# Two routers of a block with two expert layers: rows ahead of their mean, weights on four column tiles, token rows by ScalarE and GpSimd

## What is computed

```python
x = layer_norm(ALPHA * x + mix, ln_mix_g[l], ln_mix_b[l])
ffn = grouped_moe(x, router_w, router_bias, moe_w_gate[l], moe_w_up[l], moe_w_down[l])
x = layer_norm(ALPHA * x + ffn, ln_ffn_g[l], ln_ffn_b[l])

# grouped_moe
aff = jax.nn.sigmoid((x2 @ router_w).astype(jnp.float32))
sel = (aff + router_bias.astype(jnp.float32)).reshape(-1, N_GROUPS, EXPERTS_PER_GROUP)
grp_score = jnp.sum(lax.top_k(sel, 2)[0], -1)
g_idx = jnp.argmax(grp_score, -1)
...
gates = jnp.sum(jax.nn.one_hot(e_idx, N_EXPERTS, dtype=jnp.float32) * w[..., None], axis=1)
# per expert
h = jax.nn.silu(x2 @ wg_e) * (x2 @ wu_e)
return acc + (h @ wd_e) * g_e[:, None].astype(x2.dtype), None
```

## Time and profile before

| | us |
|---|---|
| median of 3 runs | 1222.84 (1222.77 to 1229.96) |
| the profiled execution | 1221.47 |
| its span | 1219.7 |
| PE busy | 1146.4 (94%) |
| DVE, ACT, POOL busy | 616.6, 457.5, 220.7 |

### The profile page before, as it was taken

One profiled execution on the slowest core, in us unless ns is written; L12 is line 12 of the kernel. 1 busy time (PEld: TensorE's weight loads), 2 busy tenths in 40 slices (PEclk: granted clock), 3 DMA queues, 4 the chain that ended last, 5 costly groups with the idle time before them and its releaser, 6 DMA issues.

```text
span 1219.7 us, 16387 instructions
## 1 busy us (share of the span) xinstructions
PE 1146.4 (94%) x6658; PEld 807.3 (66%) x6658; DVE 616.6 (51%) x880; ACT 457.5 (38%) x712; POOL 220.7 (18%) x194
## 2 busy tenths in 40 slices
PE   7999999999878998999999889999999989999998
PEld 6967644444338886644444336888887766998997
DVE  3697512122125777612222126785599884645644
ACT  3434411211024575411211016474565534434442
POOL 5500000000010000000000000377798541000000
PEclk9999899999999999799999999999999999999999
DMA  9489599999998435699999994352354331463460
GB/s 320 133 262 394 193 407 421 422 421 421 421 386 249 151 139 229 278 407 422 422 420 421 422 365 173 138 200 95 132 187 148 138 139 69 159 253 141 182 231 35
DMA packets 86884, 321.58 MB, mean 264 GB/s; under 512 B 7159, under 2 KB 18852, under 8 KB 62234
## 3 DMA queue, kind: packets, MB, share of 16 engines
q1 hardware_dynamic: 84064, 313.08, 66.2%
q0 software_dynamic: 2192, 7.23, 1.9%
q10 hardware_dynamic: 554, 0.22, 0.1%
HBM read 318.55 MB, written 1.96 MB: 263 GB/s over the span
## 4 chain that ended last, share of the span: by engine, by line
PE 63%; DVE 17%; DMA 9%; ACT 6%; issue 2%; POOL 1%; SPq 1%; DVEq 0%; ACTq 0%
PE bank L1642 32%; PE bank L1828 20%; DMA arena<-in_moe_w_up_dram 4%; DVE w_lo L699 2%; DMA arena<-in_moe_w_down_dram 2%; DMA ring<-in_w_kv_dram 2%; ACT w_hi L1058 2%; PE bank L1724 1%; PE bank L1897 1%; POOL w_lo L699 1%; SPq L807 1%; PE bank L1861 1%; PE bank L1819 1%; DVE rows L3033 1%; DVE arena L3052 1%
## 5 line engine op out<-in xcount | busy, mean ns | idle before, releaser
L699 POOL TENSOR_TENSOR w_lo<-ring,w_hi 128x512 fp32r<-128x512 f32 (+1 forms) x124 | 177.4, 1463 | 675.6 <-ACT w_hi L1058 675.6
L1058 ACT ACTIVATE w_hi<-ring 128x2048 fp32r<-128x2048 f32 (+1 forms) x102 | 191.9, 1884 | 197.8 <-PE bank L1642 196.1
L699 DVE TENSOR_TENSOR w_lo<-ring,w_hi 128x2048 fp32r<-128x2048 f32 x71 | 161.8, 2282 | 142.8 <-ACT w_hi L1058 142.8
L1642 PE MATMUL bank<-x_hi,w_hi 128*128 128x256 f32 x680 | 112.5, 288 | 2.8 <-issue 2.8
L1642 PE MATMUL bank<-x_hi,w_lo 128*128 128x256 f32 x680 | 109.7, 284 | 3.3 <-POOL w_lo L699 2.1
L1642 PE MATMUL bank<-x_lo,w_hi 128*128 128x256 f32 x680 | 109.3, 283 | 0.8 <-DVE x_lo L2389 0.7
L1828 PE MATMUL bank<-arena 128*64 128x512 f32 x352 | 98.6, 594 | 2.3 <-DMA arena<-in_moe_w_down_dram 1.8
L1642 PE MATMUL bank<-w_hi,x_hi 128*128 128x512 f32 x320 | 91.3, 399 | 6.9 <-DVE x_lo L2512 2.9
L1642 PEld LDWEIGHTS bank<-x_hi,w_hi 128*128 128x128 f32 x680 | 93.4, 191 | 5.6 <-issue 5.1
L1642 PEld LDWEIGHTS bank<-x_hi,w_lo 128*128 128x128 f32 x680 | 93.6, 191 | 3.9 <-POOL w_lo L699 2.5
L2690 DVE TENSOR_TENSOR y_r<-bank,y_r 128x512 fp32r<-128x512 f32 x32 | 22.1, 692 | 144.8 <-ACT y_r L1058 144.8
(11 more groups left out here) (363 smaller groups left out, 1626.3 us busy)
## 6 DMA issues: line engine op xcount, KB each, us to landing
ring<-in_w_in_dram SPq DMA_DIRECT2D x15, 2048.0 KB, 7.8
arena<-in_moe_w_gate_dram SPq DMA_DIRECT2D x24, 1024.0 KB, 15.2
ring<-in_moe_w_gate_dram SPq DMA_DIRECT2D x24, 1024.0 KB, 15.1
arena<-in_moe_w_down_dram SPq DMA_DIRECT2D x24, 1024.0 KB, 21.7
ring<-in_moe_w_down_dram SPq DMA_DIRECT2D x24, 1024.0 KB, 18.7
ring<-in_moe_w_up_dram SPq DMA_DIRECT2D x24, 1024.0 KB, 19.9
arena<-in_moe_w_up_dram SPq DMA_DIRECT2D x24, 1024.0 KB, 22.6
wslots<-in_moe_w_up_dram SPq DMA_DIRECT2D x16, 1024.0 KB, 17.7
```

Source lines behind the costliest of these rows:

```text
L699: last = ops.tensor_tensor(part(w_lo, label, hb)[:, x].bitcast(F32R), ring_half(label, hb)[:, x], part(w_hi, label, hb)[:, x], ALU.subtract)
L1058: return s.activation(dst, src, ACT.Copy)
L1642: last = mm(bank(use_)[0:still.shape[1], at:at + cols], still, moving, start=start and opens and (hb, n, k) == (0, 0, 0), stop=stop and cl ...
```

## The change

Nine things change.

1. Half by half. `first_half` takes the mean of the first half of a row (`mean0`) and subtracts this provisional mean from the whole row at once, and from the two means within the statistics; PE transposes the first half of a tile on that, and the second when the second half of the product has been added. The residual mean and the deviation are applied to the logits: `scales` makes the reciprocal, `less_mean` (minus mean times reciprocal) and `logit_shift`.
2. The gain of the norm goes into the router's weights (`rw` times the gain, on DVE for layer 0 and on GpSimd for layer 1, from a fresh load) and into ScalarE's copies of the gathered tokens (`gain_x` as scale). `beta_w` has four parts for two and lies in `rows[0]`.
3. The router's weights are stationary, 32 columns wide (16 are zero), on four column tiles of the array; the four partial sums are copied out (`parts`; ScalarE tile 0, DVE tile 1) and added by a matmul with `strips`.
4. ScalarE's order: root, `permuted` of tile 0, three of the four copies (before: two and then one behind the row), root, copy of the parts, an early sigmoid on one column.
5. Token rows: `permuted` writes normalized float32 rows into `rows[0]`; `tokens_high` rounds them (both tiles after the sigmoid); GpSimd's `remainders` makes the remainders in place. DVE's `remainder` is gone.
6. `gathered_first` goes by tiles: tile 0 rounded, tile 0 remainder, tile 1 rounded, tile 1 remainder.
7. `warm` ahead of the ranks has four products for two.
8. `whole_rows` has four instructions for two, and its rows come into `rows[1]`; the rows of the norm behind the experts are loaded once it is done. Three gains of the second block are loaded in the second router.
9. The last product of layer 1 takes its parts in another order, and in layer 1 the second half's residual is scaled ahead of its product.

```diff
@@ gpsimd @@
-                load_row(rows[0][:, 1, :], a["ln_mix_g"], l, "rows0")
-                load_row(mix_shift, a["ln_mix_b"], l, "rows1")
+                for k, src in enumerate((a["ln_mix_g"], a["ln_mix_b"])):
+                    load_row(rows[1][:, k, :], src, l, "rows0")
+
+            def load_rows_behind(l):
+
+                pool.wait_ge(sem("rows_out"), NT * (l + 1))
                 for k, src in enumerate((a["ln_ffn_g"], a["ln_ffn_b"])):
                     load_row(rows[1][:, k, :], src, l, "rows1")
+
+            def remainders(l):
+
+                for t in range(NT):
+                    pool.wait_ge(sem("tok_hi"), NT * l + t + 1)
+                    g.tensor_tensor(tok_lo[:, t, :].bitcast(F32R), rows[0][:, t, :], tok_hi[:, t, :], ALU.subtract)\
+                        .then_inc(sem("tok_lo"), 1)
...
             load_rows(0)
+            remainders(0)
+            load_rows_behind(0)
+            ready(pool, ("router", 0))
+            par(rw, a["router_w"].rearrange("(k p) e -> p k e", p=P), "par_router")
...
@@ scalar @@
-                s.activation(by_chunk(tok_hi[:])[:, t].bitcast(F32R), chunk_rows(res[:])[:, t], ACT.Copy,
-                             scale=rstd[:, t, 1:2]).then_inc(sem("tok_hi"), 1)
+                s.activation(by_chunk(rows[0][:])[:, t], chunk_rows(res[:])[:, t], ACT.Identity,
+                             scale=rstd[:, t, 1:2], bias=less_mean[:, t, :]).then_inc(sem("tok_rows"), 1)
+
+            def tokens_high(l, t):
+
+                act.wait_ge(sem("tok_rows"), NT * l + t + 1)
+                copy(tok_hi[:, t, :].bitcast(F32R), rows[0][:, t, :]).then_inc(sem("tok_hi"), 1)
...
                 s.activation(aff, aff, ACT.Sigmoid).then_inc(sem("affinities"), 1)
+                tokens_high(l, 0)
                 permuted(f"ln{2 * l}", 1)
+                tokens_high(l, 1)
...
                 std(name, eps_ln, (0,))
+                permuted(name, 0)
                 router_tile(name, 0, range(2))
-                permuted(name, 0)
+                router_tile(name, 1, (0,))
                 std(name, eps_ln, (1,))
-                router_tile(name, 1, (1,))
+                ready(act, ("part", l, 0))
+                free(copy(parts[:, 0, :], bank(("part", l, 0))[:, 0:P]), ("part", l, 0))
+                s.activation(ahead[:, roots[0]:roots[0] + 1], eps_ln[:], ACT.Sigmoid)
@@ tensor @@
+                def partial(t, half):
+
+                    if half == 0:
+                        claim(pe, ("part", l, t))
+                    freed(pe, (n, 2 * t + half))
+                    for k in range(4 * half, 4 * half + 4):
+                        q = slice(k % 4 * STRIP, (k % 4 + 1) * STRIP)
+                        last = mm(bank(("part", l, t))[q, 0:P], rw_wide[:, k, :], router_x(t)[:, k, :],
+                                  start=half == 0, stop=half == 1)
...
+                def whole(t):
+
+                    freed(pe, ("part", l, t))
+                    return mm(bank(("router", l))[:, t * EXPERTS:(t + 1) * EXPERTS], parts[:, t, :], strips[:, 0:EXPERTS],
+                              start=True, stop=True)
...
-                warm(("rank", l), 2)
+                warm(("rank", l), 4)
...
+                    for t in range(NT):
+                        pe.wait_ge(sem("sel"), PAIRS * l + t + 1)
+                        for n, (made, rows_) in enumerate((("tok_hi", tok_hi), ("tok_lo", tok_lo))):
+                            pe.wait_ge(sem(made), NT * l + t + 1)
...
-            out_heads(1, ..., order=[(hb, 2 * t + h) for t in range(NT) for hb in range(2) for h in range(2)])
+            out_heads(1, ..., order=[(0, 0), (0, 1), (1, 0), (1, 1), (0, 2), (1, 2), (0, 3), (1, 3)])
@@ vector @@
             for l in range(LAYERS):
-                columns = pcol[:, R_MIXB + KD * l:R_MIXB + KD * (l + 1)].unsqueeze(2)
-                v.tensor_tensor(beta_w[:, :, l, :], rw[:], bcast(columns, KD, EXPERTS), ALU.mult).then_inc(sem("beta_w"), 1)
+                for w, first in enumerate((R_MIXB, R_MIXG)):
+                    columns = pcol[:, first + KD * l:first + KD * (l + 1)].unsqueeze(2)
+                    v.tensor_tensor(beta_w[:, :, 2 * l + w, :], rw, bcast(columns, KD, EXPERTS), ALU.mult)\
+                        .then_inc(sem("beta_w"), 1)
+            dve.wait_ge(sem("beta_w"), 2 * LAYERS)
+            v.tensor_tensor(rw, rw, bcast(pcol[:, R_MIXG:R_MIXG + KD].unsqueeze(2), KD, EXPERTS), ALU.mult)\
+                .then_inc(sem("rw_gain"), 1)
...
+            def first_half(n, t):
+
+                link(half_stats(t, 0))
+                link(v.bn_aggr(mean0[:, t, :], stats[:, t, 0:1, :]))
+                v.tensor_scalar(res[:, t, :], res[:, t, :], mean0[:, t, 0:1], None, ALU.subtract)\
+                    .then_inc(sem("ahead_rows"), 1)
+                link(v.tensor_scalar(stats[:, t, 0, 1:6:3], stats[:, t, 0, 1:6:3], mean0[:, t, 0:1], None, ALU.subtract))
+                dve.wait_ge(sem("ahead_rows"), int(n[2:]) + t + 1)
...
+            def scales(n, t):
...
+                link(v.reciprocal(rstd[:, t, 1:2], rstd[:, t, 0:1]))
+                v.tensor_scalar(less_mean[:, t, :], mv[:, t, 0:1], rstd[:, t, 1:2], -1.0, ALU.mult, ALU.mult)\
+                    .then_inc(sem(f"{n}_tok"), 1)
+                dve.wait_ge(sem(f"{n}_tok"), t + 1)
+                link(v.scalar_tensor_tensor(logit_shift[:, t, :], shift_e[:, l, 1, :], less_mean[:, t, :], shift_e[:, l, 0, :],
+                                            ALU.mult, ALU.add))
...
                     select(0, t).then_inc(sem("sel"), 1)
-                remainder(f"ln{2 * l}", 1, 0)
-                for t in range(NT):
-                    remainder(f"ln{2 * l}", t, 1)
...
             for t in range(NT):
-                for half in range(2):
...
-                    if half:
-                        moments("ln2", t, last)
-                        tile_rows("ln2", t)
+                link(v.tensor_scalar(res[:, t, HALF:], xtok[:, t, HALF:], ALPHA, None, ALU.mult))
+                ready(dve, ("wo", t, 0))
...
+                if t:
+                    scales("ln2", 0)
+                freed(dve, ("wo", t, 0))
+                first_half("ln2", t)
+                ready(dve, ("wo", t, 1))
...
+                second_half("ln2", t)
```

More of the change, by code:

```diff
@@ L212, in squares @@
             return by_four[:, c % 6:c % 6 + 2, :]
-        beta_w = again_(4 * BLK + D, KD, LAYERS, EXPERTS)
+        beta_w = rows[0][:, 0, 0:2 * KD * LAYERS * EXPERTS].rearrange("p (k w e) -> p k w e", k=KD, w=2 * LAYERS)
         def shifted_rows(c):
@@ L230, in program @@
         keep = choice(NG, PER_GROUP)
+        parts = choice(NT, P)
         def router_x(t):
@@ L357, in program @@
         marks = tiny(4)
-        ahead = tiny(6)
-        shift_e = tiny(LAYERS, EXPERTS)
+        ahead = tiny(8)
+        shift_e = tiny(LAYERS, 2, EXPERTS)
         shift_x = tiny(LAYERS, KD)
+        gain_x = tiny(LAYERS, KD)
+        mean0 = tiny(NT, 2)
+        less_mean = tiny(NT, 1)
+        logit_shift = tiny(NT, EXPERTS)
         over_any = [sb(f"over_any{l}", [1, 1], I32) for l in range(LAYERS)]
@@ L423, in use_moe @@
         def use_moe(l):
-            use(("router", l), 0)
+            for t in range(NT):
+                use(("part", l, t), t)
+            use(("router", l), 2)
             use(("rank", l), 5)
@@ L1022, in _ @@
             load_rows(1)
+            remainders(1)
+            ready(pool, ("router", 1))
+            par(qg, a["q_norm_g_2"].broadcast_to([P, HD]), "par_gains")
+            par(kg, a["k_norm_g_2"].broadcast_to([P, HD]), "par_gains")
+            par(hng, a["hgrn_norm_g_2"].broadcast_to([P, VD]), "par_gains")
+            load_rows_behind(1)
             low(pool, g, FIRST_BEHIND[1], 0, pieces=4)
@@ L1744, in _ @@
             claim(pe, "shift_e")
[L1745 removed]
+            pe.wait_ge(sem("beta_w"), 2 * LAYERS)
             for k in range(KD):
[L1747 removed]
+                last = mm(bank("shift_e")[:, 0:2 * LAYERS * EXPERTS], ones[:], beta_w[:, k].rearrange("p w e -> p (w e)"),
                           start=k == 0, stop=k == KD - 1)
@@ L2132, in _ @@
             weighted(14)
-            out_heads(1, x_hi[:, 4:8, :], x_lo[:, 4:8, :], steps=during_wo1, heads={(0, 0): 2, (0, 2): 3}, order=[(hb, 2 * t + h) for t in range(NT) for hb in range(2) for h in range(2)])
+            out_heads(1, x_hi[:, 4:8, :], x_lo[:, 4:8, :], steps=during_wo1, heads={(0, 0): 2, (0, 2): 3}, order=[(0, 0), (0, 1), (1, 0), (1, 1), (0, 2), (1, 2), (0, 3), (1, 3)])
             experts(1)
@@ L2551, in whole_rows @@
+                dve.wait_ge(sem("tok_rows"), NT * (l + 1))
                 for t in range(NT):
-                    v.scalar_tensor_tensor(res[:, t, :], res[:, t, :], rstd[:, t, 1:2], mix_shift, ALU.mult, ALU.add)\
+                    last = v.scalar_tensor_tensor(res[:, t, :], res[:, t, :], mv[:, t, 0:1], rows[1][:, 0, :],
+                                                  ALU.subtract, ALU.mult)
```

(16 more changed lines are left out.)

155 lines of the change are left out of this document (71 added, 84 removed).

## The result

The changed kernel takes 1237.91 us (median of 4 runs, 1236.38 to 1240.39) for 1223.58 before (4 runs): ratio 1.012, 95% interval 1.009 to 1.015, 14.3 us slower. The forecast was +5.65.

| us | before | after | difference | forecast |
|---|---|---|---|---|
| start to end of sigmoid, layer 0 | 132.45 | 130.42 | -2.0 | -1.35 |
| sigmoid to first gate, layer 0 | 11.36 | 16.64 | +5.3 | +4.4 |
| stage, layer 0 | 219.67 | 222.34 | +2.7 | 0 |
| to the sigmoid, layer 1 | 134.67 | 134.56 | -0.1 | -0.35 |
| sigmoid to first gate, layer 1 | 12.99 | 17.40 | +4.4 | +2.95 |

A forecast was written before the change was run, and what follows sets the result against it. Expert stage taken as transfer-bound, but delayed one for one by anything ahead of its first gate product; gather ends +3.05 and +2.6 us give +5.65 on 1222.84, about 1228.5 us, range 1216.0 to 1232.5.

The forecast's parts named there:

- Step 1: Ahead of the means, layer 0: `beta_w` in five DVE instructions for two costs 0.6 us on the path.
- Step 2: DVE and ScalarE around the last product, to the sigmoid's end: router rework wins 1.35 us in layer 0, 0.35 in layer 1.
- Step 3: Choice of experts: POOL's two remainders each hold one small DVE instruction (+2.4, then due 4.9, held until 6.85); chain 4.35 us later.
- GpSimd does not hold DVE: Rival at the choice of experts: no holds, gathers end earlier, middle -4.4 us, 1218.4 us; chance 0.28.
- Step 4: First gather, 32 matmuls: 5.7 us in each layer, ending 3.05 and 2.6 us later than before.
- The clock stays up: Rival at the gather: holds exist, but it runs at 2.4 GHz throughout, +1.5 and +1.1 us, 1225.4 us; chance 0.12.
- The bounds of 4.2 and 7.6 us: Gather's duration if its 32 matmuls ran wholly at 2.4 GHz or wholly at 1.2 GHz.
- Step 5: Hidden costs: `whole_rows` 2.5 us more on DVE, scale 0 to 0.1 us a copy, POOL's extra loads; all counted as nothing.
- The extra loads of POOL come behind what they could delay: Claim that the loads moved in POOL's queue delay nothing, size 0.
- A microsecond won or lost ahead of that product moves all that follows by a microsecond: Claim that time changed ahead of the first gate product passes in full to the end, so counting stops at the gather.
- 1216.0 (no hold with a full clock, -6): Range's fast end: GpSimd holds no DVE instruction and both gathers run at 2.4 GHz, 6 us faster.

The follow-up runs named there:

- experiment 1: Changed kernel with its two token remainders per layer made by DVE behind the first selections, none by GpSimd: 1225.89 us, ratio 1.0007.

## Why the prediction was wrong

It was right where it looked and did not look far enough.

- **Step 1**, `beta_w`: +0.6 forecast, 0.2 measured (the means at 86.82 for 86.60).
- **Step 2**: tile 1 joined at 126.2 (forecast 126.6), the sigmoid ended at 130.42 (131.1). Tile 1 was joined 1.1 us later than before, for 1.5 forecast. Layer 1 won 0.1, not 0.35.
- **Step 3**, the holds: right in place, count and size. 2.42 and 2.12 us on the two instructions named, the gather at 140.24 (140.65). "GpSimd does not hold DVE" falls: with POOL's remainders gone the two took 0.29 and 0.36.
- **Step 4**, the gather: 5.83 in layer 0 (5.7); in layer 1 6.70, where "I take 5.7, as in layer 0" was 1.0 short. The holds leave PE idle for 3 us just ahead, and 514 to 518 ran at 1.2 GHz. "The clock stays up" falls for the changed kernel. Without the holds it stayed up in the gather of layer 1 in three kernels and of layer 0 in one, out of five kernels; with them in none. The bounds of 4.2 and 7.6 us were too high: in the trace its matmuls start 0.12 us apart at 2.4 GHz and 0.21 at 1.2, and with the two slower ones at its start that makes about 4.1 and 7.1.
- **Step 5 is what failed.** "The extra loads of POOL come behind what they could delay" asked which instruction stands behind them in POOL's queue. It should have asked what the transfer engines carry at 152 us. The prediction itself said that the stage is bound by transfers, at a share of 1.01, and then let 1.05 MB a layer move into it for nothing. From the same rows, 1.05 / 0.416 = 2.5 us a layer, the forecast would have been 1233.5. The runs show 3 to 6 us for taking them out and 6.7 for putting them in; in the traces the last block of weights lands 3.3 us earlier and 3.7 later for both layers together.
- **The end of the stage** had no term at all. In layer 1 the last `gate` and `down` products ran in part at 1.2 GHz, which made the rest behind the last block 2.3 us longer (13.7 for 11.4). No run shows that this belongs to the change: kernels with late rows have it or not, and so have those with early ones. The 2.3 us are part of the profiled difference of 16.4; their part in the 14.3 of the medians is not known.
- Step 5's scale: "0 to 0.1 us on each" was right in size (0.096), but it priced only the four copies ahead of the first gate product, not those of the later pairs, 0.36 us a pair. What hides them is the stream of weights: +0.5 us in the two stages of the kernel before together.
- "A microsecond won or lost ahead of that product moves all that follows by a microsecond" held: 10.5 us won there in experiment 1 shortened the span by 10.1.
- The lower end of the range, "1216.0 (no hold with a full clock, -6)", is 1216.9 by its own terms (-2.8 and -3.1).

The 14.3 us by the single repairs, in medians: 11.6 for the holds with what they do to the gather, 3.0 for the loads. The copies' share can't be told from nothing beside them.

## What to carry to other kernels

A load that is moved costs nothing only if the transfer engines have room at its new place. In a stretch that transfers bound, price it as bytes written over the stream's rate, less what the stream can make up. Before a longer stage is put down to an edit, split it at the landing of its last load and read the granted clock of what follows: here up to 2.3 us of it came and went with the clock and not with the edit. Before giving GpSimd a piece of work, look at what DVE does beside it: a DVE instruction with two SBUF inputs can wait for the whole GpSimd instruction (2.1 us here). So cut it short, or give the work to DVE where it waits anyway.

## What the runs showed of the hardware

- A row broadcast to 128 partitions reads 4 KB and takes the stream's time for the 512 KB that it writes: the 1.05 MB moved late in the kernel before cost the weights 1.2 MB by 20 us and 0.7 MB at 180, and the last block landed 1.8 and 1.9 us later.
- A hold ends with the GpSimd instruction: 0.29 us became 2.4 beside 1024 columns and 0.8 beside 256.
- The same product of 32 matmuls behind a wait for weights took 7.1 us at a granted clock of 1.00 and 8.6 to 8.8 where the mean was 0.81 to 0.82, with early rows as with late ones.
- The gather of 32 matmuls took 3.8 us from first to last at a granted clock of 1.00 and 6.4 where most of it ran at 0.50; a 3 us pause of PE ahead of it was followed by half the clock within the next 3 us, though the clock still read 1.00 during the pause.
